# Four-layer block plus a second network on one core: in layer B, queries are scaled in the scores and rotated on VectorE, and the keys' sums of squares become two fp32r products, issued two tiles after their tile

## The chip, the cores and the metric

One core of one Trainium2 chip runs the whole program. The metric is the device time of one execution in microseconds (us); less is better. Engines: TensorE (PE, matrix products), VectorE (DVE), ScalarE (ACT), GpSimd (POOL) and SyncE (SP, which issues loads). Each works through its own instructions in order, and they hold each other back with counting semaphores.

## The reference, cut to what matters

The program computes two networks, one behind the other, on 512 tokens of width 1024. The change is in the first one's second layer, called B here: a norm, a projection, a query and key norm, partial rotation (the first 32 of 128 dimensions), attention in three groups of different windows, a gate and an output projection.

```python
def mixer_b(h, w_in, q_gain, k_gain, w_out):
    proj = h @ w_in
    qkv = proj[..., :n_qkv].reshape(bsz, S, 3, N_B_GROUPS, B_HEADS, HEAD_DIM)
    z = proj[..., n_qkv:]
    for g, (window, dilation) in enumerate(B_PATTERNS):
        q = apply_partial_rotary(rms_norm(qkv[:, :, 0, g], q_gain[g]), cos, sin)
        k = apply_partial_rotary(rms_norm(qkv[:, :, 1, g], k_gain[g]), cos, sin)
        o, lse = dilated_window_attention(q, k, qkv[:, :, 2, g], window // dilation, dilation)
    ...
    y = o.reshape(bsz, S, B_WIDTH).astype(h.dtype) * jax.nn.silu(z)
    return y @ w_out
```

rms_norm divides a vector of 128 by the root of its mean square and multiplies it with a gain. The root differs by token and head, the gain by dimension.

## The kernel before, in words

All order is written out by hand, one function for each engine. Layer B runs over i = 0 to 3, each a pair of heads. One i has these parts:

- **Twelve query and key tiles**, t = 0 to 11, with t = 4g + 2w + f: g is the group, w is 0 for queries and 1 for keys, f the head. A tile is [128 dimensions, 512 tokens], made by PE as 24 products of 512 columns in PSUM bank t mod 3 (`tile_f`; lines L558 to L560 of `mm3`: each fp32 product is three fp32r products of a high and a low part). ACT squares the tile into `sq` (L1538) and copies it to `tmp` (L1543). Behind the next tile, PE sums the squares over the 128 dimensions with one fp32 product against a matrix of ones (`ssq`, L803), ACT takes the root (L1530), DVE its reciprocal (L2154), multiplies tile, gain and reciprocal (L2159), and starts the rotation: a shuffle of 32 partitions and a product with the sine table (L2168, L2170). POOL ends it (`rope`, L420, L423).
- **Values**, six tiles of 48 products of 256 columns.
- **Attention units** n = 0 to 7, each 128 queries of one head. PE makes the scores (L843, L845). DVE adds the mask and takes the row maximum in one instruction (L2184), negates it (L2187), ACT takes the exponential (L1556), DVE divides by its sum (L2191, L2193), PE transposes the weights (`flip`, L854), ACT copies them out of PSUM (`turned`, L1566), and PE multiplies with the values (`far` L867, `close` L874). A value tile (n up to 3) or a gate tile (n = 4, 6) stands between. The last two flips stand behind tiles 0 and 1 of the next i.

ACT also writes the high part of the weights (`Wh`, L1339), POOL the low part (`Wl`, L366), two panels ahead of PE; a panel serves two tiles. SP loads the raw weights into three buffers.

## Time and profile before

| what | value |
|---|---|
| median of 3 runs | 3163.09 us (3161.67 to 3164.63) |
| the profiled execution | 3160.02 us, its span 3158.3 us |
| busy: PE, DVE, ACT, POOL | 98%, 50%, 35%, 49% of the span |
| chain that ended last, by engine | PE 92%, DVE 4%, ACT 1%, issue 1%, POOL 1%, DMA 1% |
| granted PE clock, mean | 0.992 |

The span is first to last instruction, and 1.7 us lie around it. The profiled execution is 3.1 us below the median. A granted clock of 1.00 is TensorE's level of 2.4 GHz, 0.50 that of 1.2 GHz. In the rows further down a matmul's duration runs until its last result, so that the durations of neighbours overlap; the distance of two starts tells what one costs a busy PE. An fp32 product has two records, an fp32r product or a transpose one.

### The profile page before, as it was taken

The numbers are of one execution on the slowest core, as the hardware profiler recorded it, in microseconds if no ns is written. First come the engines' busy times: TensorE is split into PE (matmuls) and PEld (weight loads), VectorE is DVE, ScalarE is ACT, GpSimd is POOL, SyncE is SP. The second block draws the span as 40 slices with busy tenths as digits, with TensorE's granted clock in tenths as the row PEclk, the third lists the DMA queues.
The fourth block names the chain that finished last, engine by engine and source line by source line (L and its number), as shares of the span: only waits on it lengthen the run. The fifth ranks groups of instructions, "written<-read, shape, count | busy, mean of one in ns | idle before, by whom it ended". The sixth has DMA issues, their size and how long they took to land.

```text
span 3158.3 us, 38137 instructions
## 1 busy us (share of the span) xinstructions
PE 3097.0 (98%) x15692; PEld 2524.9 (80%) x15692; DVE 1582.0 (50%) x2066; ACT 1100.3 (35%) x1445; POOL 1552.3 (49%) x1138
## 2 busy tenths in 40 slices
PE   8999999999999999999999999899999999999998
PEld 6888878788888888878887888676888787778887
DVE  6654475838473525355466777654211356542113
ACT  3322244444443423332223444434222343242222
POOL 4444475748473555454444422236445556354453
PEclk9999999999999999999999999899999999999999
DMA  5544322222222323355443111112333242223331
GB/s 199 169 156 159 135 83 80 80 67 81 67 81 76 98 94 103 106 185 177 136 160 117 54 41 41 41 54 94 94 106 94 81 147 80 80 67 94 105 95 67
DMA packets 270975, 319.26 MB, mean 101 GB/s; under 512 B 6850, under 2 KB 228689, under 8 KB 270482
## 3 DMA queue, kind: packets, MB, share of 16 engines
q1 hardware_dynamic: 232768, 247.48, 24.2%
q10 hardware_dynamic: 38034, 69.34, 6.5%
q8 instruction: 125, 2.05, 0.3%
q14 instruction: 48, 0.39, 0.0%
HBM read 310.50 MB, written 6.29 MB: 100 GB/s over the span
## 4 chain that ended last, share of the span: by engine, by line
PE 92%; DVE 4%; ACT 1%; issue 1%; POOL 1%; DMA 1%; ACTq 0%; SPq 0%; DVEq 0%
PE ps L558 26%; PE ps L560 25%; PE ps L559 25%; PE psx L803 1%; PE psx L1091 1%; PE ps L1122 1%; PE ps L629 1%; PE psx L782 1%; PE psx L1251 1%; PE ps L597 1%; PE psx L845 1%; POOL Wl L366 1%; PE ps L593 1%; DVE stD L2354 1%; PE ps L594 1%
## 5 line engine op out<-in xcount | busy, mean ns | idle before, releaser
L366 POOL TENSOR_TENSOR Wl<-Wr,Wh 128x512 fp32r<-128x512 f32 x928 | 1271.5, 1402 | 1407.9 <-ACT Wh L1339 1403.8
L558 PE MATMUL ps<-Ah,Wh 128*128 128x512 f32 x1944 | 778.1, 400 | 0.0
L560 PE MATMUL ps<-Ah,Wl 128*128 128x512 f32 x1944 | 757.5, 390 | 0.0
L559 PE MATMUL ps<-Al,Wh 128*128 128x512 f32 x1944 | 757.3, 390 | 0.0
L1339 ACT ACTIVATE Wh<-Wr 128x2048 fp32r<-128x2048 f32 x232 | 443.1, 1910 | 349.6 <-DMA Wr<-in_w_mlp_in_dram 109.6
L558 PEld LDWEIGHTS ps<-Ah,Wh 128*128 128x128 f32 x1944 | 365.1, 188 | 84.8 <-issue 12.0
L559 PEld LDWEIGHTS ps<-Al,Wh 128*128 128x128 f32 x1944 | 365.1, 188 | 81.9 <-issue 8.9
L560 PEld LDWEIGHTS ps<-Ah,Wl 128*128 128x128 f32 x1944 | 364.8, 188 | 77.3
L558 PE MATMUL ps<-Yh,Wh 128*128 128x512 f32 x1088 | 426.0, 392 | 0.1
L559 PE MATMUL ps<-Yl,Wh 128*128 128x512 f32 x1088 | 423.8, 390 | 0.0
L560 PE MATMUL ps<-Yh,Wl 128*128 128x512 f32 x1088 | 423.7, 389 | 0.0
L558 PEld LDWEIGHTS ps<-Yh,Wh 128*128 128x128 f32 x1088 | 204.6, 188 | 44.0 <-issue 0.8
L560 PEld LDWEIGHTS ps<-Yh,Wl 128*128 128x128 f32 x1088 | 204.5, 188 | 42.8
L559 PEld LDWEIGHTS ps<-Yl,Wh 128*128 128x128 f32 x1088 | 204.5, 188 | 41.9
L558 PE MATMUL ps<-Wh,Ah 128*128 128x256 f32 (+1 forms) x688 | 220.7, 321 | 2.2 <-DVE vA L2078 2.2
L2070 DVE SCALAR_TENSOR_TENSOR macc<-modw,sc,macc 128x512 f32<-128x512 f32 x168 | 163.5, 973 | 113.0 <-DMA modw<-in_w_mod_dram 106.6
L559 PE MATMUL ps<-Wl,Ah 128*128 128x256 f32 (+1 forms) x688 | 215.1, 313 | 0.0
L560 PE MATMUL ps<-Wh,Al 128*128 128x256 f32 (+1 forms) x688 | 215.0, 312 | 0.0
L2154 DVE RECIPROCAL rs<-rs 128x512 f32<-128x512 f32 x48 | 160.6, 3346 | 37.8 <-ACT rs L1530 37.8
L2437 DVE TENSOR_TENSOR tmp<-tmp 128x512 f32<-128x512 f32 x64 | 52.2, 816 | 201.2 <-ACT tmp L1807 201.2
L558 PEld LDWEIGHTS ps<-Wh,Ah 128*128 128x128 f32 x688 | 131.1, 191 | 13.8 <-issue 5.5
L559 PEld LDWEIGHTS ps<-Wl,Ah 128*128 128x128 f32 x688 | 131.1, 191 | 9.2 <-issue 1.9
(408 smaller groups left out, 3893.8 us busy)
## 6 DMA issues: line engine op xcount, KB each, us to landing
Wr<-in_a_w_in_dram SPq DMA_DIRECT2D x48, 1024.0 KB, 6.3
modw<-in_w_mod_dram ACTq DMA_DIRECT2D x96, 512.0 KB, 5.4
Wr<-in_b_w_in_dram SPq DMA_DIRECT2D x40, 1024.0 KB, 5.0
Wr<-in_w_mlp_in_dram SPq DMA_DIRECT2D x32, 1024.0 KB, 5.5
Wr<-in_w_mlp_out_dram SPq DMA_DIRECT2D x32, 1024.0 KB, 5.1
Wr<-in_a_w_out_dram SPq DMA_DIRECT2D x16, 1024.0 KB, 5.1
Wr<-in_c_w_in_dram SPq DMA_DIRECT2D x16, 1024.0 KB, 5.4
Wr<-in_attn_w_qkv_dram SPq DMA_DIRECT2D x12, 1024.0 KB, 5.1
```

The source lines that it names most:

```text
L366: last = pool.tensor_tensor(E.Wl[:, s, part], E.Wr[:, s, part], E.Wh[:, s, part].bitcast(F32), ALU.subtract)
L558: pe.matmul(o, ah, bh, start=first, stop=False)
L559: pe.matmul(o, ah, bl, start=False, stop=False)
L560: return pe.matmul(o, al, bh, start=False, stop=last)
L593: pe.matmul(bank[b], part(E.Wh, p, k, f * P, f * P + P, KD), Ah[:, k, :], start=(k == 0), stop=False)
L594: pe.matmul(bank[b], part(E.Wl, p, k, f * P, f * P + P, KD), Ah[:, k, :], start=False, stop=False)
L597: m = pe.matmul(bank[b], part(E.Wh, p, k, f * P, f * P + P, KD), Al[:, k, :], start=False, stop=(k == KD - 1))
L629: pe.matmul(bank[t], Ah[:, a, t * P:(t + 1) * P], part(W, p, k, 0, S, TT), start=(a == 0 and W is E.Wh), stop=False)
L1339: act.activation(E.Wh[:, s, :], E.Wr[:, s, :], ACT.Copy).then_inc(*HI.did(p))
L2070: dve.scalar_tensor_tensor(t, w, E.sc2[:, k, who:who + 1], t, ALU.mult, ALU.add).then_inc(*V.did("mac", L, nb, who, k))
L2154: dve.reciprocal(rs[:, r, :], rs[:, r, :]).then_inc(*V.did())
L2437: dve.tensor_tensor(t, t, t, ALU.mult).then_inc(*V.did(L, "sqr", iq, c))
```

## The change

**Queries.** Their tile is multiplied by the gain alone, on ACT, straight into `QB`. Rotation runs wholly on DVE (`turn_query`). For a group, the squares of both heads are summed at once behind tile 4g + 2 by eight narrow fp32 products (`query_sums`), whose result has one row of sums for each of four blocks of 128 tokens. ACT takes the root (`query_roots`), PE transposes it behind tile 4g + 3 (`columns`), DVE takes the reciprocal of 128x4 numbers (`rate`), and the attention units multiply the scores with it. So the fused mask and maximum becomes three multiply-adds and a separate maximum.

**Keys.** The square is split into an fp32r high part (ACT, `rsR`, the memory of `rs`) and low part (DVE, `square_low`), and two fp32r products sum them (`key_sum`), behind tile t + 2 rather than t + 1. Root, reciprocal, scaling (`scaled`) and rotation (`turn_key`, then POOL) follow as before. Keys 10 and 11 of an i have places of their own: `key_sum(10)` behind tile 11, `key_sum(11)` behind the first value tile. On DVE key t is scaled in the step of tile t + 3 (10 and 11: one step later).

```diff
-    E.ones, E.ident = sb("ones", [P, P]), sb("ident", [P, P])
+    E.onesR, E.ident = sb("onesR", [P, P], F32R), sb("ident", [P, P])
+    E.ones = E.onesR[:].bitcast(F32)
...
+    E.rsR, = phase(("rsR", [P, 2, S], F32R))
     E.rs = sb("rs", [P, 2, S])
+    E.sqR, = phase(("sqR", [P, 2, S], F32R))
     E.sq = sb("sq", [P, 2, S])
...
-            t = 0
             for g in range(3):
-                for qk in range(2):
-                    for f in range(2):
-                        if t:
-                            rope(i, t - 1)
-                        if f == 0:
-                            ahead("B", "qk", i, g, qk)
-                        t += 1
+                ahead("B", "qk", i, g, 0)
+                if g:
+                    rope(i, 4 * g - 2)
+                ahead("B", "qk", i, g, 1)
+                if g:
+                    rope(i, 4 * g - 1)
             for g in range(3):
+                if g == 0:
+                    rope(i, 10)
...
-        def ssq(i, t):
-            r = t % 2
-            into(4 + r)
-            pe.wait_ge(*A.of("B", "sq", i, t))
-            pe.matmul(psx[:, r, :], ones[:], sq[:, r, :], start=True, stop=True).then_inc(*X.did("B", "ssq", i, t))
-            emptied[4 + r] = A.of("B", "sqrt", i, t)
+        def key_sum(i, t):
+            b = 5 - t % 2
+            into(b)
+            pe.wait_ge(*V.of("B", "sl", i, t))
+            pe.matmul(bank[b], E.onesR[:], E.rsR[:, t % 2, :], start=True, stop=False)
+            pe.matmul(bank[b], E.onesR[:], E.sqR[:, t % 2, :], start=False, stop=True).then_inc(*X.did("B", "ssq", i, t))
+            emptied[b] = A.of("B", "sqrt", i, t)
+
+        def query_sums(i, g):
+            into(4)
+            pe.wait_ge(*A.of("B", "sq", i, 4 * g + 1))
+            for f in range(2):
+                for q in range(TT):
+                    m = pe.matmul(psx[32 * q:32 * q + 32, 0, f * P:(f + 1) * P], ones[:, 0:32], sq[:, f, q * P:(q + 1) * P], start=True, stop=True)
+            m.then_inc(*X.did("B", "ssq", i, 4 * g))
+            emptied[4] = V.of("B", "rq", i, g)
+
+        def columns(i, g):
+            pe.wait_ge(*A.of("B", "sqrt", i, 4 * g))
+            for f in range(2):
+                m = pe.transpose(psx[:, 0, (2 + f) * P:(3 + f) * P], rs[:, 1, f * P:(f + 1) * P], ident[:])
+            m.then_inc(*X.did("B", "rt", i, g))
...
-            if t:
-                ssq(i, t - 1)
+            if t % 4 == 2:
+                query_sums(i, t // 4)
+            elif t % 4 == 3:
+                if t == 11:
+                    key_sum(i, 10)
+                columns(i, t // 4)
+            elif t >= 4:
+                key_sum(i, t - 2)
...
+                pe.wait_ge(*V.of("B", "turned", i, 8 + hh))
...
-        def sqrt(i, t):
-            r = t % 2
+        def key_root(i, t):
             act.wait_ge(*X.of("B", "ssq", i, t))
-            if t >= 2:
-                act.wait_ge(*V.of("B", "qk", i, t - 2))
-            act.activation(rs[:, r, :], psx[:, r, :], ACT.Sqrt, bias=eps[:, 0:1], scale=1.0 / P).then_inc(*A.did("B", "sqrt", i, t))
+            act.activation(rs[:, t % 2, :], psx[:, 1 - t % 2, :], ACT.Sqrt, bias=eps[:, 0:1], scale=1.0 / P).then_inc(*A.did("B", "sqrt", i, t))
+
+        def query_roots(i, g):
+            act.wait_ge(*X.of("B", "ssq", i, 4 * g))
+            if g:
+                act.wait_ge(*V.of("B", "qk", i, 4 * g - 1))
+            act.activation(rs[:, 1, 0:2 * P], psx[:, 0, 0:2 * P], ACT.Sqrt, bias=eps[:, 0:1], scale=1.0 / P).then_inc(*A.did("B", "sqrt", i, 4 * g))
 
         def qk(i, t):
+            g, f = t // 4, t % 2
             act.wait_ge(*T.of("B", "qk", i, t))
-            if t >= 2:
+            if is_key(t):
+                act.wait_ge(*X.of("B", "ssq", i, 4 * g))
+            elif t >= 4:
                 act.wait_ge(*X.of("B", "ssq", i, t - 2))
             elif i:
                 act.wait_ge(*V.of("B", "y", 0, 2 * (i - 1)))
-            act.activation(sq[:, t % 2, :], ps[t % 3][:], ACT.Square).then_inc(*A.did("B", "sq", i, t))
-            if t >= 3:
-                act.wait_ge(*V.of("B", "qk", i, t - 3))
-            elif i:
-                act.wait_ge(*X.of("B", "pv", i - 1, 0))
-            act.activation(tmp[:, t % 3, :], ps[t % 3][:], ACT.Copy).then_inc(*A.did("B", "cp", i, t))
-            if t % 2 == 0:
-                ahead("B", "qk", i, t // 4, t // 2 % 2)
+            act.activation(sq[:, f, :], ps[t % 3][:], ACT.Square).then_inc(*A.did("B", "sq", i, t))
+            if is_key(t):
+                n = 2 * g + f
+                act.wait_ge(*A.of("B", "sq", i, t))
+                if f:
+                    act.wait_ge(*X.of("B", "rt", i, g))
+                elif t >= 4:
+                    act.wait_ge(*V.of("B", "qk", i, t - 4))
+                act.activation(E.rsR[:, f, :], sq[:, f, :], ACT.Copy).then_inc(*A.did("B", "sh", i, t))
+                if n >= 3:
+                    act.wait_ge(*V.of("B", "qk", i, 4 * ((n - 3) // 2) + 2 + (n - 3) % 2))
+                elif i:
+                    act.wait_ge(*X.of("B", "pv", i - 1, 0))
+                act.activation(tmp[:, n % 3, :], ps[t % 3][:], ACT.Copy).then_inc(*A.did("B", "cp", i, t))
+            else:
+                if i and t == 0:
+                    act.wait_ge(*X.of("B", "s", i - 1, 7))
+                act.activation(E.QB[:, g, f, :], ps[t % 3][:], ACT.Identity, scale=pk(E, "b_q_gain", g)).then_inc(*A.did("B", "cp", i, t))
+            if f == 0:
+                ahead("B", "qk", i, g, t // 2 % 2)
...
-                if t:
-                    sqrt(i, t - 1)
                 qk(i, t)
+                if t % 4 == 2:
+                    query_roots(i, t // 4)
+                elif t == 11:
+                    key_root(i, 10)
+                elif t >= 4 and t % 4 < 2:
+                    key_root(i, t - 2)
...
-        def rest(i, t):
-            g, qk, f, r = t // 4, t // 2 % 2, t % 2, t % 2
-            dst = (KB if qk else QB)[:, g, f, :]
+        def square_low(i, t):
+            r = t % 2
+            dve.wait_ge(*A.of("B", "sh", i, t))
+            dve.tensor_tensor(E.sqR[:, r, :], sq[:, r, :], E.rsR[:, r, :].bitcast(F32), ALU.subtract).then_inc(*V.did("B", "sl", i, t))
+
+        def rq(g, f):
+            return stB[:, B_UNITS + 2 * g + f, :]
+
+        def rate(i, g):
+            dve.wait_ge(*X.of("B", "rt", i, g))
+            for f in range(2):
+                dve.reciprocal(rq(g, f), psx[:, 0, (2 + f) * P:(3 + f) * P].rearrange("p (q n) -> p q n", q=TT)[:, :, 0]).then_inc(*V.did("B", "rq", i, g))
+
+        def scaled(i, t):
+            n, r = t // 4 * 2 + t % 2, t % 2
             dve.wait_ge(*A.of("B", "sqrt", i, t))
             dve.reciprocal(rs[:, r, :], rs[:, r, :]).then_inc(*V.did())
             dve.wait_ge(*V.now())
             dve.wait_ge(*A.of("B", "cp", i, t))
-            if i and t == 0:
-                dve.wait_ge(*X.of("B", "s", i - 1, 7))
-            dve.scalar_tensor_tensor(dst, tmp[:, t % 3, :], pk(E, "b_k_gain" if qk else "b_q_gain", g), rs[:, r, :],
+            dve.scalar_tensor_tensor(KB[:, t // 4, t % 2, :], tmp[:, n % 3, :], pk(E, "b_k_gain", t // 4), rs[:, r, :],
                                      ALU.mult, ALU.mult).then_inc(*V.did("B", "qk", i, t))
+
+        def turn_key(i, t):
             dve.wait_ge(*V.of("B", "qk", i, t))
-            if t >= 2:
-                dve.wait_ge(*G.of("B", "rope", i, t - 2))
-            elif i and t == 0:
+            if t >= 4:
+                dve.wait_ge(*G.of("B", "rope", i, t - 4))
+            elif i and t == 2:
                 dve.wait_ge(*X.of("B", "pv", i - 1, 0))
-            swapped = (acc if r else tmp[:, 3, :])[0:32, :]
+            swapped = (acc if t % 2 else tmp[:, 3, :])[0:32, :]
             pinned()
-            dve.stream_shuffle(swapped, dst[0:32, :], SWAP).then_inc(*V.did("B", "swap", i, t))
+            dve.stream_shuffle(swapped, KB[0:32, t // 4, t % 2, :], SWAP).then_inc(*V.did("B", "swap", i, t))
             dve.wait_ge(*V.of("B", "swap", i, t))
             dve.tensor_tensor(swapped, swapped, ropeB[:, 1, :], ALU.mult).then_inc(*V.did("B", "rp", i, t))
+
+        def turn_query(i, t):
+            q, swapped = QB[0:32, t // 4, t % 2, :], PB[0:32, 0, :]
+            dve.wait_ge(*A.of("B", "cp", i, t))
+            if i and t == 0:
+                dve.wait_ge(*X.of("B", "flip", i - 1, 6))
+            dve.wait_ge(*V.now())
+            pinned()
+            dve.stream_shuffle(swapped, q, SWAP).then_inc(*V.did())
+            dve.wait_ge(*V.now())
+            dve.tensor_tensor(swapped, swapped, ropeB[:, 1, :], ALU.mult).then_inc(*V.did())
+            dve.tensor_tensor(q, q, ropeB[:, 0, :], ALU.mult).then_inc(*V.did())
+            dve.wait_ge(*V.now())
+            dve.tensor_tensor(q, q, swapped, ALU.add).then_inc(*V.did("B", "turned", i, t))
...
-            pinned()
-            dve.tensor_tensor_reduce(PB[:, u % 2, :], psx[:, u % 2, :], maskB[:, u % 4, :], 1.0, 10 * NEG,
-                                     ALU.add, ALU.max, stB[:, u, 0:1]).then_inc(*V.did("B", "sc", i, u))
+            if u % 4 == 0:
+                dve.wait_ge(*V.of("B", "rq", i, 2))
+            for g, c0, c1 in ((0, 0, 256), (1, 256, 384), (2, 384, 512)):
+                dve.scalar_tensor_tensor(PB[:, u % 2, c0:c1], psx[:, u % 2, c0:c1], rq(g, u // 4)[:, u % 4:u % 4 + 1], maskB[:, u % 4, c0:c1],
+                                         ALU.mult, ALU.add).then_inc(*V.did("B", "sc", i, u))
             dve.wait_ge(*V.of("B", "sc", i, u))
+            dve.tensor_reduce(stB[:, u, 0:1], PB[:, u % 2, :], AX.X, ALU.max).then_inc(*V.did("B", "mx", i, u))
+            dve.wait_ge(*V.of("B", "mx", i, u))
...
-            for t in range(11):
-                rest(i, t)
-                if i and t == 1:
+            for t in range(13):
+                if t % 4 == 3:
+                    rate(i, t // 4)
+                if t < 12:
+                    if is_key(t):
+                        square_low(i, t)
+                    else:
+                        turn_query(i, t)
+                k = t - 1 if t > 10 else t - 3
+                if k >= 2 and is_key(k):
+                    scaled(i, k)
+                    turn_key(i, k)
+                if i and t == 2:
                     y(i - 1, 1)
-            rest(i, 11)
```

DVE around tile 5 of head pair 0, before (`rs` reciprocal, scaling, shuffle, sine product of one tile each):

```order
280 L2154 RECIPROCAL rs<-rs 128x512 [waits act]
281 L2159 SCALAR_TENSOR_TENSOR QB<-tmp,PK,rs 128x512 [waits act,dve]
282 L2168 STREAM_SHUFFLE tmp<-QB 32x512 [waits dve,pool]
283 L2170 TENSOR_TENSOR tmp<-tmp,ropeB 32x512 [waits dve]
284 L2154 RECIPROCAL rs<-rs 128x512 [waits act]
285 L2159 SCALAR_TENSOR_TENSOR QB<-tmp,PK,rs 128x512 [waits act,dve]
```

The same place after the change, from the turning of query tile 5 to the scaling of key tile 3:

```order
281 L2246 STREAM_SHUFFLE PB<-QB 32x512 [waits act,dve]
282 L2248 TENSOR_TENSOR PB<-PB,ropeB 32x512 [waits dve]
283 L2249 TENSOR_TENSOR QB<-QB,ropeB 32x512
284 L2251 TENSOR_TENSOR QB<-QB,PB 32x512 [waits dve]
285 L2221 RECIPROCAL rs<-rs 128x512 [waits act]
286 L2224 SCALAR_TENSOR_TENSOR KB<-tmp,PK,rs 128x512 [waits act,dve]
287 L2235 STREAM_SHUFFLE tmp<-KB 32x512 [waits dve]
288 L2237 TENSOR_TENSOR tmp<-tmp,ropeB 32x512 [waits dve]
289 L2208 TENSOR_TENSOR sqR<-sq,rsR 128x512 [waits act]
290 L2221 RECIPROCAL rs<-rs 128x512 [waits act]
291 L2224 SCALAR_TENSOR_TENSOR KB<-tmp,PK,rs 128x512 [waits act,dve]
```

Keys 2 and 3 are now scaled behind query tile 5, with the split of key 6's square between them, and queries have no reciprocal of 512 columns.

ACT after the change, at tile 6 of head pair 0 (root of key 3, then square, high part and copy of key 6, a weight panel's high part, and the root of group 1's queries):

```order
150 L1558 ACTIVATE rs<-psx,eps 128x512 [waits aux]
151 L1575 ACTIVATE sq<-ps 128x512 [waits aux,tile]
152 L1583 ACTIVATE rsR<-sq 128x512 [waits dve,act]
153 L1588 ACTIVATE tmp<-ps 128x512
154 L1370 ACTIVATE Wh<-Wr 128x2048 [waits raw1]
155 L1564 ACTIVATE rs<-psx,eps 128x256 [waits dve,aux]
```

PE after the change, at the end of tile 7, where before one fp32 product `L803 ... 128x512` stood:

```order
1834 L567 MATMUL ps<-Al,Wh 128x512
1835 L568 MATMUL ps<-Ah,Wl 128x512
1836 L827 MATMUL psx<-ident,rs 128x128 [waits act]
1837 L827 MATMUL psx<-ident,rs 128x128
1838 L566 MATMUL ps<-Ah,Wh 128x512 [waits act,lo]
```

The root of group 1's queries (row 155 of ACT) waits for DVE's scaling of key 3, whose reciprocal lies in the same memory, and PE's transposes (row 1836) wait for that root.

## Rows read from the trace of the kernel before

**Rows 1.** Windows, layer B: busy us and count of each engine, granted clock, DMA.

```profile
421.00:1022.00 601.00, 599.43 (x3486) 495.82 (x3487) 370.34 (x447) 260.00 (x391) 376.05 (x268) 1.00 0.23 76
```

**Rows 2.** Waits of TensorE (PE) in layer B: total us, times, longest.

```profile
PE psx L854 <- DVE PB L2193: 1.1, 4, 0.3
```

**Rows 3.** Timeline of PE, head pair 0: start us, us, what.

```profile
434.11 1.02 PE L803 MATMUL psx<-sq,ones 128*128 128x512 f32 x2
...
435.20 0.40 PE L559 MATMUL ps<-Al,Wh 128*128 128x512 f32 x1
...
440.46 1.02 PE L803 MATMUL psx<-sq,ones 128*128 128x512 f32 x2
```

**Rows 4.** Timeline of PE at full clock: narrow fp32 products, then transposes.

```profile
2146.12 0.64 PE L678 MATMUL psx<-sq,ones 128*32 128x128 f32 x16
2146.69 1.98 PE L1005 MATMUL psx<-hsF,tabF 128*128 128x512 f32 x4
...
546.54 0.60 PE L854 MATMUL psx<-ident,PB 128*128 128x128 f32 x4
546.98 0.61 PE L867 MATMUL ps<-PTB,VB 128*128 128x128 f32 x4
```

**Rows 5.** Timeline of ScalarE (ACT), head pair 0.

```profile
454.21 0.69 ACT L1530 ACTIVATE rs<-psx,eps 128x512 f32<-128x512 f32 x1 [4.68 <-PE psx L803]
454.79 0.59 ACT L1538 ACTIVATE sq<-ps 128x512 f32<-128x512 f32 x1
455.27 0.60 ACT L1543 ACTIVATE tmp<-ps 128x512 f32<-128x512 f32 x1
```

**Rows 6.** Timeline of VectorE (DVE), head pair 0.

```profile
484.21 1.02 DVE L2159 SCALAR_TENSOR_TENSOR QB<-tmp,PK,rs 128x512 f32<-128x512 f32 x1
...
486.20 0.68 DVE L2170 TENSOR_TENSOR acc<-acc,ropeB 32x512 f32<-32x512 f32 x1
486.81 3.33 DVE L2154 RECIPROCAL rs<-rs 128x512 f32<-128x512 f32 x1
```

**Rows 7.** Groups of DVE: count, busy us, mean ns, idle before.

```profile
L2154 DVE RECIPROCAL rs<-rs 128x512 f32<-128x512 f32 x48 | 160.6, 3346 | 37.8 <-ACT rs L1530 37.8
L2023 DVE TENSOR_TENSOR Yl<-tmp,Yh 128x512 fp32r<-128x512 f32 x112 | 88.6, 791 | 58.9 <-ACT Yh L1813 46.2 <-ACT Yh L1650 11.2
L2354 DVE TENSOR_REDUCE stD<-psx 128x2 f32<-128x1536 f32 x32 | 56.2, 1755 | 34.2 <-PE psx L1091 34.2
...
L2159 DVE SCALAR_TENSOR_TENSOR QB<-tmp,PK,rs 128x512 f32<-128x512 f32 x24 | 26.9, 1123 | 0.9
```

**Rows 8.** Tile QB: min/median/max ns of one.

```profile
L2159 DVE SCALAR_TENSOR_TENSOR QB<-tmp,PK,rs x24: 750/1018/1868, 427.6 to 909.7; 128x512 f32<-128x512 f32 x24
```

**Rows 9.** Attention unit 4: DVE's first step, then PE's transposes.

```profile
534.33 0.69 DVE L2184 CUSTOM_DVE_ANT_0 PB<-psx,maskB 128x512 f32<-128x512 f32 x1 [4.67 <-PE psx L845]
...
536.93 0.63 PE L854 MATMUL psx<-ident,PB 128*128 128x128 f32 x4 [0.28 <-DVE PB L2193]
```

**Rows 10.** ACT's copy of unit 6 and PE's product that reads it.

```profile
558.03 0.60 ACT L1566 ACTIVATE PTB<-psx 128x512 f32<-128x512 f32 x1
...
561.75 0.61 PE L867 MATMUL ps<-PTB,VB 128*128 128x128 f32 x4
```

**Rows 11.** PE after long and short waits, and the granted clock of 2 us.

```profile
2018.46 2.26 PE L1091 MATMUL psx<-KD,QD 64*128 64x512 f32 x8 [3.02 <-ACT rs L1737]
2020.65 2.52 PE L1122 MATMUL ps<-tmp,VD 128*128 128x128 f32 x12
...
2020.00:2022.00 2.00, 2.00 (x10) 1.35 (x7) 1.24 (x1) 0.00 (x0) 0.00 (x0) 0.50 0.89 231
...
2051.12 1.13 PE L1161 MATMUL ps<-woF,hdX 64*128 64x512 f32 x2 [1.41 <-DVE kcF L2382]
2052.30 1.56 PE L1091 MATMUL psx<-KD,QD 64*128 64x512 f32 x8
...
2055.33 1.50 PE L1122 MATMUL ps<-tmp,VD 128*128 128x128 f32 x12
```

More of the change, by code:

```diff
@@ L2035, in preamble @@
     def preamble():
[L2036 removed]
+        dve.memset(E.acc[:], 1.0).then_inc(*V.did())
+        dve.wait_ge(*V.now())
+        dve.tensor_copy(E.onesR[:], E.acc[:, 0:P]).then_inc(*V.did("ones"))
         dve.memset(eps[:], EPS).then_inc(*V.did("eps"))
```

20 lines of the change are left out of this document (11 added, 9 removed).

## Prediction

> **What bounds the kernel now.** I read the page first: the chain that ended last lies almost wholly on PE. Then the windows, for the stretch that the change touches: in the 601 us of layer B, PE is busy for 599.4 at a granted clock of 1.00, while DVE has 370 us of work and POOL 376 [rows 1]. Then the waits: the largest one of PE there is the flip that waits for DVE's division, 1.1 us over four times [rows 2]. So nothing but PE's own instructions sets the time of this layer. Work taken from PE there is time gained, us for us, and a wait put on PE is time lost in the same way. Work taken from DVE, ACT or POOL gains nothing by itself.
>
> **Keys: one fp32 product becomes two fp32r ones.** Two sums start 6.35 us apart (434.11 and 440.46). From the tile's second product at 435.20 to the next sum are 23 products in 5.26 us [rows 3], 0.229 each, so a tile is 5.49 and one fp32 sum 0.86. Two fp32r products of the same 512 columns are 0.46. There are 24 keys: 24 x 0.40 = **9.6 us gained**.
>
> **Queries.** A group loses two fp32 sums, 1.72 us. It gets eight fp32 products with 32 result rows and 128 columns, for which the norm has the very form: eight took from 2146.12 to 2146.69, 0.57 us at full clock. It also gets two transposes; four took 0.44 us (546.54 to 546.98) [rows 4], so 0.22. Saved 0.93, and 12 groups give **11.1 us gained**. The preamble's fp32r ones and the moved mask load lie beside loads and the layer's norm, and I cost them at nothing; if all of the one copy of 128 columns showed, it would be under 1 us [rows 8].
>
> **The new wait behind tile 7 and tile 11.** The transposes of group g wait for the root of the queries' sums. That root waits (g at least 1) until DVE has scaled key 4g - 1. I follow this from the end of tile 5 (e5 = 0), in the order that the listing of DVE after the change shows.
>
> - PE: key sum 0.46, tile 6 5.49, query sums 0.57, tile 7 5.49. PE is at the transposes at **12.0**.
> - ACT: after the key sum's last result (0.46 + 0.16 until it has drained) come square and copy of query 5, started 0.48 apart and the last 0.60 long [rows 5]: the copy is there at 1.70.
> - DVE turns query 5: shuffle and sine product as before, cosine product and sum new. Before, 0.97 lay between a multiplication's end (485.23) and the sine product (486.20), and 0.61 from there to the next start [rows 6]. I split the 0.97 into a wait of DVE for itself, 0.20, and a shuffle of 0.77; a product that the next one waits for I take at its 0.68 and 0.07 of latency. I take 0.77 + 0.61 + 0.75 + 0.61 = 2.74, so 4.44.
> - DVE scales key 2: reciprocal 3.35 and 0.04 of latency, multiplication 1.12 [rows 7]: 8.95. It rotates it: from the multiplication's end at 485.23 to the next reciprocal at 486.81 are 1.58 [rows 6]: 10.53.
> - It splits the square of key 6, a subtraction to fp32r as L2023, 0.79 [rows 7], of which 0.75 until the next starts: 11.28. (ACT's high part waits for key 2's scaling at 8.95, and is there in time.)
> - It scales key 3: 3.36 and 1.12, so 15.76. ACT takes the root of 256 columns; 512 take 0.69 [rows 5], I take 0.50 and 0.08 of latency: **16.34**.
>
> PE waits 16.34 - 12.0 = 4.3 us behind tile 7. Behind tile 11 the same chain runs from the end of tile 9, and PE has one key sum more (0.46): 3.9 us. Queued behind the waiting transposes is everything that PE has, next the tile after. Group 0 has no such wait, since its root waits for no key. Four i make 4 x 8.2 = **32.9 us lost**. The bounds of one wait: with the shortest multiplication (0.75 [rows 8]) for both multiplications and the subtraction it is 3.6 and 3.1; with the longest (1.87) for the three it is 6.9 and 6.4. I take the means, since POOL runs beside DVE here as before. Over four i: 27 to 53 us.
>
> The Trainium skill (GPSIMD Engine Reference, Key points) says that GpSimd shares its SBUF interfaces with VectorE and that instructions with two SBUF inputs contend. By that rule the spread from 0.75 to 1.87 is POOL's doing, and the change takes the queries' rotations from POOL. With the shortest durations throughout, the lost time would be 27.
>
> **The clock after such waits.** PE waited 3.02 us before 2018.46, and then the granted clock was 0.50, the level of 1.2 GHz: the scores took 2.26 and the products after them 2.52, where the same took 1.56 and 1.50 at full clock [rows 11]. That is 1.7 us lost. After a wait of 1.41 (2051.12) the next scores took 1.56, so the clock held [rows 11]. The new waits are longer than 3, and full-size products follow, so I expect a fall each time. A part of it should lie inside the longer wait, so I take 1.35 for each, between 0 and 1.7: 8 x 1.35 = **10.8 us lost** (0 to 14).
>
> The Trainium skill (TensorE: Matmul & The Clock Gate, What's actually happening) says that the throttled clock is the default and that activity releases it. By it, too, idle time costs more than its own length; without it the sum would be 10.8 lower.
>
> **Attention units.** The fused instruction took 0.69 for 512 columns [rows 9]; a maximum over 1536 columns took 1.755 [rows 7]. That is 1.04 ns a column and 0.16 fixed. Three pieces are then 1.01, the wait of DVE for itself 0.20, the maximum 0.69: 1.9 instead of 0.7, less 0.1 in which the pieces overlap, so **1.1 us longer**, bounds 0.8 and 1.6. Most units have a tile beside them on PE. The flip of unit 4 has not: it stood 0.28 us waiting already [rows 9], so here all of it shows: 4 x 1.1 = **4.4 us lost**. Units 6 and 7 together make ACT's copies at the head of the next i some 2.0 later, and PE comes 0.86 sooner, since the sum behind tile 1 is gone. The copy that started at 558.03 ended 3.1 us before PE's product at 561.75 [rows 10], so 0.2 is left. I cost it at 0, with up to 2 us for three such places.
>
> **The sum**, against the profiled execution: 3160.0 - 9.6 - 11.1 + 32.9 + 10.8 + 4.4 = 3187.4, that is +27.4. The runs' median is 3.1 above that execution, so 3190.5 in its terms.
>
> **What lies beside the path.** DVE has in a group two turned queries (5.5), two splits (1.6), two scaled and rotated keys (12) and the small reciprocals, under 20 us, against some 24 of PE: it is not the bound, only late in its order. ACT gets a copy for each key (0.6). POOL loses 48 of its 96 rotation steps and keeps the weights' low parts; it waits more for keys, but a panel has over 20 us. SP's queue is not touched. The values behind tile 11 hide key 11: its sum stands one value tile behind, and two more follow before unit 0 needs it.
>
> **The rivals.**
>
> - The waits, but no fall of the clock (0.12). PE's work before and after is dense. Against it: 3.02 us sufficed once. Time 3190.5 - 10.8 = 3179.7.
> - The chain on DVE is longer than its means (0.14). For it: key 3's multiplication falls where POOL makes a panel's low part. Time: +15 to +20 for waits near the upper bound, near 3208.
> - **Faster** (0.08): the chain never stands on PE's path. It is one mechanism: key 3 scaled before PE is at the transposes. That needs a chain 4.3 us shorter, as if DVE scaled key 2 ahead of query 5, whose copy comes 1.7 us after its tile while DVE idles. The order rows speak against it. Time 3163.1 - 20.7 + 4.4 = 3146.8. It decides at a wait of 16.3 / 8 = 2.0 us: below that, with no fall of the clock, the kernel is faster.
> - The waits come out between (0.05), about 2 us each, and the change cancels: 3163.
>
> **How the numbers follow.** The forecast itself gets 0.61; its own range is 3180 to 3202 (waits 4 us more or less over an i, clock 0 to 14). For 8 in 10 I go from 3170, the no-fall case with the shortest chain, to 3209. A difference of 0.2%, 6.3 us, is about the least that can be told from none here. Slower by more than that: 0.61 + 0.12 + 0.14 and a little of the cases between, 0.88. Faster 0.08, same 0.04.
>
> **What would show it.** In the profile after: eight waits of PE on ACT's root in front of the transposes, about 4 us each, none in group 0; granted clock under 1.00 after them in layer B; key sums at 0.46 and query sums at 0.57 to 0.6; four waits of a flip on DVE near 1.4. Wrong if those eight waits are under 2 us, or if the clock stays at 1.00.

## The result, and the profile after

Before, the kernel took 3163.86 us (median of 4 runs, 3161.67 to 3167.15), after the change 3211.82 us (4 runs, 3211.60 to 3213.44): a ratio of 1.0155, 95% interval 1.0142 to 1.0167. The change makes it **slower by 48.0 us**. I had forecast slower by 27.4, with a range up to 3209. The sign was right and the size was not: the time lies outside the range. The profiled execution of after took 3213.44 us (span 3211.7). The same kernel in a later comparison took 3207.88 beside 3166.17, which is 41.7 us slower; that time would lie just inside the range.

The page of after, engines' busy time and the shares of the chain that ended last:

```profile
PE 3104.2 (97%) x15860; PEld 2539.0 (79%) x15860; DVE 1590.4 (50%) x2179; ACT 1109.1 (35%) x1457; POOL 1489.9 (46%) x1090
...
PE 88%; DVE 7%; issue 1%; ACT 1%; POOL 1%; DMA 1%; ACTq 0%; SPq 0%; DVEq 0%
```

Before, 92% of the chain was PE's and 4% DVE's; now it is 88% and 7%. So the end now depends on DVE's work in places where it depended on PE's. To place them, I take the norm's products with ones, which stand once at the end of each part of the program, and read when they start. First before, then after (PE's timeline: start, us, line, operation; a count under x20 means only that the window asked for ended inside the group, and the start is not touched by it):

```profile
400.64 2.39 PE L649 MATMUL psx<-ones,ident 128*128 128x128 f32 x20
...
1022.48 2.39 PE L649 MATMUL psx<-ones,ident 128*128 128x128 f32 x20
...
1335.56 2.39 PE L649 MATMUL psx<-ones,ident 128*128 128x128 f32 x20
...
2766.86 1.39 PE L649 MATMUL psx<-ones,ident 128*128 128x128 f32 x11
```

```profile
402.41 2.39 PE L657 MATMUL psx<-onesR,ident 128*128 128x128 f32 x20
...
1067.25 1.95 PE L657 MATMUL psx<-onesR,ident 128*128 128x128 f32 x16
...
1380.34 1.83 PE L657 MATMUL psx<-onesR,ident 128*128 128x128 f32 x15
...
2821.09 2.17 PE L657 MATMUL psx<-onesR,ident 128*128 128x128 f32 x18
```

From the first row to the second is layer B: 621.8 us before, 664.8 after, so **43.0 us longer**. From the third row to the fourth no line of the program differs, yet it is 1431.3 before and 1440.8 after. Most of that isn't the change: the same kernel's second profile has 1431.8 there, and the kernels of the experiments lie anywhere from 1432 to 1441. It goes with the time for which the granted clock stood at its lower level in this stretch: 44.4 us in after, 23.9 in its second profile. So profiled spans differ by some 9 us outside of layer B, and I compare layer B. (Some 3 us may be the change's even so, see the end of the part on the prediction.)

PE's waits in layer B of after (waiting tile and line, who releases it: us in all, times, longest):

```profile
PE psx L827 <- ACT rs L1564: 36.9, 8, 5.6
PE psx L885 <- DVE PB L2278: 4.5, 4, 1.1
PE psx L811 <- DVE sqR L2208: 2.6, 4, 0.7
```

Where [rows 2] had 1.1 us of waiting over four flips, there are eight waits of the transposes (L827) on the root of the queries' sums (L1564), 36.9 us, up to 5.6 each. They stand behind tile 7 and tile 11, for the four i, and none in group 0, as forecast. The flips wait 4.5, or 1.12 each, where I had said near 1.4. Not forecast: the sum of key 10 waits 0.65 four times for the split of its square on DVE.

PE's timeline of after in the first i shows the terms that I had priced (sums L811 and L820, transposes L827; tiles left out):

```profile
428.80 0.65 PE L820 MATMUL psx<-sq,onesR 128*32 128x128 f32 x16
...
435.00 0.38 PE L827 MATMUL psx<-ident,rs 128*128 128x128 f32 x2
...
440.71 0.39 PE L811 MATMUL psx<-rsR,onesR 128*128 128x512 f32 x1
...
446.64 0.39 PE L811 MATMUL psx<-rsR,onesR 128*128 128x512 f32 x1
...
452.65 0.64 PE L820 MATMUL psx<-sq,onesR 128*32 128x128 f32 x16
...
464.58 0.69 PE L827 MATMUL psx<-ident,rs 128*128 128x128 f32 x2 [5.57 <-ACT rs L1564]
```

From one key sum to the next (440.71 to 446.64) are 5.93 us where [rows 3] had 6.35: 0.42 gained, 24 times 10.1. The query sums and the tile behind them take 6.20 (428.80 to 435.00), the two transposes and a tile 5.71 (435.00 to 440.71), a key sum and a tile 5.93. The end of tile 5 is at 446.64, tile 6 and the key sum end at 452.65, and the transposes of group 1 start at 464.58, after 5.57 us of waiting.

What was late is read from DVE, ACT and POOL in the same stretch (rows of after's timeline, DVE first):

```profile
448.74 0.73 DVE L2246 STREAM_SHUFFLE PB<-QB 32x512 f32<-32x512 f32 x1
449.50 1.28 DVE L2248 TENSOR_TENSOR PB<-PB,ropeB 32x512 f32<-32x512 f32 x1
...
452.03 3.33 DVE L2221 RECIPROCAL rs<-rs 128x512 f32<-128x512 f32 x1
455.39 0.75 DVE L2224 SCALAR_TENSOR_TENSOR KB<-tmp,PK,rs 128x512 f32<-128x512 f32 x1
...
456.69 0.73 DVE L2235 STREAM_SHUFFLE tmp<-KB 32x512 f32<-32x512 f32 x1 [0.37 <-issue]
...
458.06 1.77 DVE L2208 TENSOR_TENSOR sqR<-sq,rsR 128x512 fp32r<-128x512 f32 x1
459.77 3.33 DVE L2221 RECIPROCAL rs<-rs 128x512 f32<-128x512 f32 x1
463.14 0.82 DVE L2224 SCALAR_TENSOR_TENSOR KB<-tmp,PK,rs 128x512 f32<-128x512 f32 x1
```

```profile
456.24 0.64 ACT L1583 ACTIVATE rsR<-sq 128x512 fp32r<-128x512 f32 x1 [2.21 <-DVE KB L2224]
...
464.05 0.48 ACT L1564 ACTIVATE rs<-psx,eps 128x256 f32<-128x256 f32 x1 [4.88 <-DVE KB L2224]
```

```profile
457.50 1.79 POOL L428 TENSOR_TENSOR KB<-KB,ropeB 32x512 f32<-32x512 f32 x1 [7.26 <-DVE tmp L2235]
...
460.93 5.84 POOL L374 TENSOR_TENSOR Wl<-Wr,Wh 128x512 fp32r<-128x512 f32 x4
```

Key 3's multiplication (463.14, 0.82) ends at 463.96, ACT takes the root at 464.05, PE's transposes follow. Backwards from there: key 3's reciprocal starts at 459.77 because the split before it took 1.77 us, with POOL's rotation of key 2 (457.50 to 459.29) beside it. The sine product at 449.50 took 1.28 where others take 0.68.

The granted clock over this wait (windows of 2 us; columns: length, busy us and instructions of PE, PEld, DVE, ACT, POOL, then mean granted clock, DMA share, GB/s):

```profile
460.00:462.00 2.00, 0.00 (x0) 0.00 (x0) 2.00 (x1) 0.00 (x0) 2.00 (x2) 1.00 0.88 284
462.00:464.00 2.00, 0.00 (x0) 0.00 (x0) 1.92 (x2) 0.00 (x0) 2.00 (x3) 0.54 0.68 240
464.00:466.00 2.00, 1.42 (x5) 1.23 (x6) 1.64 (x5) 1.60 (x4) 2.00 (x2) 0.50 0.00 0
466.00:468.00 2.00, 2.00 (x6) 1.57 (x5) 1.29 (x1) 0.48 (x1) 2.00 (x2) 0.50 0.00 0
468.00:470.00 2.00, 2.00 (x8) 1.58 (x7) 0.00 (x0) 0.00 (x0) 1.73 (x2) 0.75 0.04 8
```

PE stands from 459.01 to 464.58. The clock is still 1.00 in the first 3 us of that, 0.54 and 0.50 from 462 on, and 1.00 again at 469. PE's products from 464.58 on run at the level of 1.2 GHz for 4.4 us. Over layer B I added up the windows of 0.5 us: PE is busy for 2.7 to 6.1 us at the low level behind each of the eight waits, and half of that, **17.3 us**, is lost. Another 1.7 us are lost in the norm at the layer's start (407.6 to 411.0), behind none of these waits; the second profile lacks them and loses 16.8, all behind the eight. So the clock takes 19.0 in all here. Before, it stood at 1.00 in all of layer B.

Together in layer B: 18.6 gained by the cheaper sums, 39.5 lost by waits (36.9 + 2.6), 3.4 by the flips (4.5 less 1.1), 19.0 by the clock. That is +43.3, against 43.0 read.

### The profile page after: what moved, and what is told of

It reads as the page before. It is cut to its first block, busy times and chain, and to the rows that moved or that the text cites. A ratio compares the mean times of both kernels' runs of the same rounds, so it can differ in the third digit from the quotient of the medians.

```text
span 3211.7 us, 38480 instructions
## 1 busy us (share of the span) xinstructions
PE 3104.2 (97%) x15860; PEld 2539.0 (79%) x15860; DVE 1590.4 (50%) x2179; ACT 1109.1 (35%) x1457; POOL 1489.9 (46%) x1090
## 3 DMA queue, kind: packets, MB, share of 16 engines
q1 hardware_dynamic: 232768, 247.48, 23.9%
q8 instruction: 126, 2.06, 0.3%
## 4 chain that ended last, share of the span: by engine, by line
PE 88%; DVE 7%; issue 1%; ACT 1%; POOL 1%; DMA 1%; ACTq 0%; SPq 0%; DVEq 0%
PE ps L566 25%; PE ps L568 24%; PE ps L567 24%; DVE rs L2221 2%; PE psx L1122 1%; PE ps L1153 1%; PE ps L637 1%; PE psx L790 1%; PE psx L1282 1%; PE psx L876 1%; PE ps L605 1%; PE psx L874 1%; PE ps L601 1%; POOL Wl L374 1%; PE ps L602 1%
## 5 line engine op out<-in xcount | busy, mean ns | idle before, releaser
L566 PE MATMUL ps<-Ah,Wh 128*128 128x512 f32 x1944 | 770.1, 396 | 1.2 <-DVE vA L2133 1.2
L568 PEld LDWEIGHTS ps<-Wh,Al 128*128 128x128 f32 x688 | 134.2, 195 | 7.6
```

The lines of the kernel that those rows point to most:

```text
L566: pe.matmul(o, ah, bh, start=first, stop=False)
L568: return pe.matmul(o, al, bh, start=False, stop=last)
```

## The experiments

Two theories stood at first. The main one: PE's loss is a wait on DVE's in-order work, which the change makes PE depend on because the queries' root is written into the memory of a key's reciprocal, and the low clock behind each wait. The rival: DVE's order alone is at fault, since query 5 stands ahead of key 2.

**The root in memory of its own.** The queries' root of groups 1 and 2 goes into a tile that holds the gate later, so it doesn't wait for key 4g - 1 to be scaled. ACT's rows have only the waits that the other tile needs: the high part of keys 7 and 11, too, no longer waits for the transposes (not shown below).

```diff
-                m = pe.transpose(psx[:, 0, (2 + f) * P:(3 + f) * P], rs[:, 1, f * P:(f + 1) * P], ident[:])
+                m = pe.transpose(psx[:, 0, (2 + f) * P:(3 + f) * P], (E.szB[:] if g else rs[:, 1, :])[:, f * P:(f + 1) * P], ident[:])
...
-            if g:
-                act.wait_ge(*V.of("B", "qk", i, 4 * g - 1))
-            act.activation(rs[:, 1, 0:2 * P], psx[:, 0, 0:2 * P], ACT.Sqrt, bias=eps[:, 0:1], scale=1.0 / P).then_inc(*A.did("B", "sqrt", i, 4 * g))
+            if g == 1 and i:
+                act.wait_ge(*V.of("B", "y", 0, 2 * i - 1))
+            elif g == 2:
+                act.wait_ge(*X.of("B", "rt", i, 1))
+            act.activation(E.szB[:, 0:2 * P] if g else rs[:, 1, 0:2 * P], psx[:, 0, 0:2 * P], ACT.Sqrt, bias=eps[:, 0:1], scale=1.0 / P).then_inc(*A.did("B", "sqrt", i, 4 * g))
```

> The root of the queries' sums of groups 1 and 2 goes to memory of its own, so it no longer waits for the scaling of key 4g - 1; nothing else changes. Theory 1 (the eight waits on this root, and the clock that falls behind them, are the loss): the 37 us of waits and about 17 us of clock go, granted clock in layer B 1.00, time near 3158 (between 3153 and 3165). Rival (VectorE's whole work in a group is what PE waits for, and the root is only the place where it shows): the waits come back at the key sums or at the tiles' banks, and at least half of the 54 us stays, time above 3180.

Measured: 3170.11 (10 runs, 3166.21 to 3176.55), 1.0021 of before (1.0012 to 1.0030). 41.7 of the 48 us are gone by the medians, and layer B is 628.3. So most of the loss hangs on the shared memory, and the rival falls with the next kernel. But the time is 12 us above the 3158 that I expected (7.5 above before), and the waits of PE say why:

```profile
PE psx L811 <- ACT szB L1566: 11.2, 4, 3.1
PE psx L885 <- DVE PB L2280: 4.5, 4, 1.1
```

The wait for DVE moved, in part, to the sum of key 10. The profile names ACT's root (L1566) for it, but nothing in `key_sum` waits for that root. It waits for the split of the key's square on DVE, which ends at the same time: in the first i at 484.08, the root at 484.12. PE goes on 0.15 behind the split, as in after (491.15 and 491.30). With one more such wait of 1.0 and 2.3 on the root itself PE waits 14.5 in front of these sums and transposes, where it was 39.5, and the clock still loses 6.3 us. That part is what the rival of my expectation had said. DVE was late by its two-input steps. PE, then the timeline of DVE, then POOL:

```profile
484.23 0.47 PE L811 MATMUL psx<-rsR,onesR 128*128 128x512 f32 x1 [1.90 <-ACT szB L1566]
```

```profile
467.84 1.81 DVE L2251 TENSOR_TENSOR QB<-QB,ropeB 32x512 f32<-32x512 f32 x1
...
474.22 1.76 DVE L2251 TENSOR_TENSOR QB<-QB,ropeB 32x512 f32<-32x512 f32 x1
...
482.33 1.75 DVE L2210 TENSOR_TENSOR sqR<-sq,rsR 128x512 fp32r<-128x512 f32 x1
...
609.91 6.74 DVE L2251 TENSOR_TENSOR QB<-QB,ropeB 32x512 f32<-32x512 f32 x1
```

```profile
609.51 1.62 POOL L431 TENSOR_TENSOR KB<-KB,acc 32x512 f32<-32x512 f32 x1
611.10 5.01 POOL L374 TENSOR_TENSOR Wl<-Wr,Wh 128x512 fp32r<-128x512 f32 x4
```

In the first i, products over 32x512 that take 0.68 to 0.72 elsewhere take 1.47 to 1.81, beside POOL's work. In each of the other three i the cosine product of query 8 takes 6.74 to 6.75 us. It starts while POOL adds, lasts through POOL's next four steps, which take 1.27 to 1.28 each (others of them take up to 1.8), and ends 0.5 us after the last of them. These three steps stand ahead of the three waits of 3.1. Why a step is held up for one of POOL's steps here and for five there, no run shows.

**Only DVE's order.** The scaling and rotation of key t - 3 are issued ahead of the query, the shared memory stays.

```diff
             for t in range(13):
+                k = t - 1 if t > 10 else t - 3
+                if k >= 2 and is_key(k):
+                    scaled(i, k)
+                    turn_key(i, k)
                 if t % 4 == 3:
...
-                k = t - 1 if t > 10 else t - 3
-                if k >= 2 and is_key(k):
-                    scaled(i, k)
-                    turn_key(i, k)
```

> In each step VectorE scales and rotates the key before it turns the query or splits a square, rather than after. Memory and waits are as in the changed kernel. Theory 1 with the order on VectorE as the cause: the root is there 5 us sooner, so the eight waits shrink from 3.9 to 5.6 us to at most 1 each and the clock stays at 1.00: 3160 to 3168. Rival (length of VectorE's work): the waits stay above 3 us each and the time above 3195.

Measured: 3209.54 (3207.14 to 3218.74), 1.0152 (1.0135 to 1.0169), layer B 666.7. PE's waits:

```profile
PE psx L811 <- DVE sqR L2208: 30.7, 8, 5.8
PE psx L827 <- ACT rs L1564: 11.9, 4, 3.0
```

42.6 us of waits instead of 39.5. The root's waits fell from 36.9 to 11.9, and the key sums now wait 30.7 for the split, which the early scaling pushed back. The clock loses 16.9. So the order is not the cause by itself: whichever of DVE's steps stands last is the one PE waits for.

**PE kept busy before the waits.** Sixteen products that nobody reads stand in front of the transposes of groups 1 and 2. They cost PE nearly what it waits, so they show what the clock alone takes.

```diff
         def columns(i, g):
+            if g:
+                into(3)
+                for k in range(16):
+                    pe.matmul(bank[3], part(E.Wh, E.at["B", "qk", i, g, 1], k % KD, 0, P, KD), Ah[:, k % KD, :], start=True, stop=True)
```

> Before the transposes of groups 1 and 2, PE makes 16 products of 512 columns into an unused bank (3.7 us, no one reads them), so that the wait is filled with work. The root still comes when it came. Theory 1: the waits shrink by 3.7 each, the clock stays at 1.00, and only the clock's part is gained: 3211.8 - 17 = 3195 (3192 to 3199). Rival (the low clock costs next to nothing, the waits are all): 3209 to 3213.

Measured: 3195.28 (3191.84 to 3198.79), 1.0101 (1.0086 to 1.0116), as expected; layer B 650.6. The windows view over nearly all of it:

```profile
424.00:1052.00 628.00, 612.46 (x3774) 514.87 (x3773) 377.05 (x558) 266.19 (x401) 315.31 (x220) 1.00 0.22 73
```

The granted clock is 1.00 as a mean, 1.7 us are lost to it instead of 19.0, and the kernel is 16.5 us faster (14.2 in layer B) with products that do nothing. The waits on the root fell from 36.9 to 8.4. By these numbers the products cost about 31.6 of PE's time, an estimate (28.5 + 17.3 less 14.2), so 3 more than they took off the waits. The Trainium skill (TensorE: Matmul & The Clock Gate, What's actually happening) says that TensorE is throttled by default and released by activity; this trace agrees, by those 16.5 us.

**The scores not scaled.** The three scaled pieces and their maximum go back to one fused instruction. This kernel leaves out the queries' scale.

```diff
-            for g, c0, c1 in ((0, 0, 256), (1, 256, 384), (2, 384, 512)):
-                dve.scalar_tensor_tensor(PB[:, u % 2, c0:c1], psx[:, u % 2, c0:c1], rq(g, u // 4)[:, u % 4:u % 4 + 1], maskB[:, u % 4, c0:c1],
-                                         ALU.mult, ALU.add).then_inc(*V.did("B", "sc", i, u))
+            pinned()
+            dve.tensor_tensor_reduce(PB[:, u % 2, :], psx[:, u % 2, :], maskB[:, u % 4, :], 1.0, 10 * NEG,
+                                     ALU.add, ALU.max, stB[:, u, 0:1]).then_inc(*V.did("B", "sc", i, u))
```

> The attention units keep the fused mask and maximum of the kernel before, so the queries' scale is left out of the scores; all else is the changed kernel. Theory 1: the flip of unit 4 waits 0.28 instead of 1.12 us, four times, so 3.4 us less: 3208.4 (3206 to 3210). Rival (the longer units cost more than that wait, by delaying the next head pair): 6 to 12 us less, below 3206.

Measured: 3200.46 (3195.20 to 3204.17), 1.0112 (1.0095 to 1.0129). The time is 8 us below what I expected, and lies in the rival's band. Layer B is 658.8, so 6.1 less: the flips wait 0.28 again, four times, which is the 3.4 of my sum, and the clock loses 15.2 instead of 19.0. The waits on the root are 36.8 as in after, so the rival's delay of the next head pair isn't there. The rest of the 11 us lies outside of layer B, where executions differ without a change. So 3.4 is shown for the flips, and no more.

**Key rotation on POOL cut to one column.** One execution. This kernel leaves out all but one column of the cosine product and sum of the keys.

```diff
-        pool.tensor_tensor(q, q, E.ropeB[:, 0, :], ALU.mult).then_inc(*G.did("B", "cos", i, t))
+        pool.tensor_tensor(q[:, 0:1], q[:, 0:1], E.ropeB[:, 0, 0:1], ALU.mult).then_inc(*G.did("B", "cos", i, t))
...
-        pool.tensor_tensor(q, q, spare, ALU.add).then_inc(*G.did("B", "rope", i, t))
+        pool.tensor_tensor(q[:, 0:1], q[:, 0:1], spare[:, 0:1], ALU.add).then_inc(*G.did("B", "rope", i, t))
```

> The changed kernel, in which POOL's two steps of the keys' rotation work on one column instead of 512 (so the keys' rotation is left out for the rest). Theory 1 with contention between VectorE and POOL in two-input steps: the subtraction that splits a key's square behind a rotation takes 0.7 instead of 1.8 us, and the eight root waits shrink by about 1 us each, to about 29 in all. Rival (the subtraction to fp32r takes 1.3 to 1.8 by itself): waits and durations unchanged.

Measured: 3205.54, layer B 661.6. The split of a square (by its tile: shortest, median and longest in ns), first in after, then in this kernel:

```profile
L2208 DVE TENSOR_TENSOR sqR<-sq,rsR x24: 692/1292/1789, 433.4 to 955.7; 128x512 fp32r<-128x512 f32 x24
```

```profile
L2208 DVE TENSOR_TENSOR sqR<-sq,rsR x24: 671/693/1765, 431.8 to 951.0; 128x512 fp32r<-128x512 f32 x24
```

The median falls from 1292 to 693 ns when POOL has next to nothing to do beside it. So the contention is shown for this step. The Trainium skill (GPSIMD Engine Reference, Key points) says that instructions of VectorE with two SBUF inputs contend with GpSimd; the trace agrees. The 2.6 us of waits for key 10's split are gone. But PE's waits on the root did not fall, they sum to 39.0 (8 times, up to 5.1), and my 29 was wrong. The chain's other two-input step took the delay over. DVE and then POOL, one i later:

```profile
608.91 0.67 DVE L2208 TENSOR_TENSOR sqR<-sq,rsR 128x512 fp32r<-128x512 f32 x1
...
612.88 1.79 DVE L2224 SCALAR_TENSOR_TENSOR KB<-tmp,PK,rs 128x512 f32<-128x512 f32 x1
```

```profile
610.42 5.38 POOL L374 TENSOR_TENSOR Wl<-Wr,Wh 128x512 fp32r<-128x512 f32 x4 [0.79 <-ACT Wh L1370]
```

The split takes 0.67 now, but POOL comes to the low parts of a weight panel at 610.42 instead of 613.07, and key 3's multiplication, which lies among them, takes 1.79 instead of 0.82. An overlap doesn't always slow DVE: in after the same multiplication lies beside the same weights' low parts (460.93 on) and takes 0.82, while the four of POOL take 5.84 instead of 5.38. Which of the two is slowed I can't predict from these rows.

**Three variants on top of the root's own memory.** Each is compared with its 3170.11, layer B 628.3.

The query's cosine product and sum go to POOL, as they were before the change:

```diff
+                rope(i, 4 * g)
+                rope(i, 4 * g + 1)
...
-            dve.tensor_tensor(swapped, swapped, ropeB[:, 1, :], ALU.mult).then_inc(*V.did())
-            dve.tensor_tensor(q, q, ropeB[:, 0, :], ALU.mult).then_inc(*V.did())
-            dve.wait_ge(*V.now())
-            dve.tensor_tensor(q, q, swapped, ALU.add).then_inc(*V.did("B", "turned", i, t))
+            dve.tensor_tensor(swapped, swapped, ropeB[:, 1, :], ALU.mult).then_inc(*V.did("B", "rp", i, t))
```

> As e1_own (roots in memory of their own), and the queries' cosine product and sum go back to POOL. Layer B took 628.3 us in e1_own, 6.5 above before, with 11 us of waits on the key sums of keys 10 that came late from VectorE. Theory 1 (VectorE is late because its two-input steps of 32x512 take up to 1.8 us beside POOL): two such steps less for each query, the waits fall under 3 us, the clock stays at 1.00, layer B 612 to 618. Rival (POOL becomes late with the weights' low parts or the keys' rotation): PE waits on POOL, layer B above 628.

Measured: 3159.72 (10 runs, 3151.73 to 3161.45), 0.9982 (0.9972 to 0.9992), layer B 612.5, as expected. The waits of key 10's sum are gone, and no step of the queries' turn is longer than 1.80. I had expected less than 3 us of waits; what is left is the flips and, 1.0 each time, the sum of key 11:

```profile
PE psx L886 <- DVE PB L2281: 4.5, 4, 1.1
PE psx L813 <- DVE sqR L2211: 4.1, 4, 1.0
```

The keys' sum as one fp32 product again, with no split on DVE:

```diff
-            pe.wait_ge(*V.of("B", "sl", i, t))
-            pe.matmul(bank[b], E.onesR[:], E.rsR[:, t % 2, :], start=True, stop=False)
-            pe.matmul(bank[b], E.onesR[:], E.sqR[:, t % 2, :], start=False, stop=True).then_inc(*X.did("B", "ssq", i, t))
+            pe.wait_ge(*A.of("B", "sq", i, t))
+            pe.matmul(bank[b], ones[:], sq[:, t % 2, :], start=True, stop=True).then_inc(*X.did("B", "ssq", i, t))
```

> As e1_own, but keys are summed by one fp32 product of 0.86 us again, at the new place two tiles behind; the high and low parts of the squares are gone from ACT and VectorE. Theory 1: PE loses 24 x 0.40 = 9.6 us, and gains the 11 us of waits and 6 of clock back, since VectorE has 24 subtractions of 1.3 us less and ACT no longer waits for a key's scaling: layer B 619 to 623. Rival (the fp32r products are worth their VectorE work): layer B above 628.

Measured: 3163.38 (10 runs, 3154.71 to 3164.45), 0.9995 (0.9985 to 1.0005), layer B 616.1, a little better than expected. It gives back the 10 us that the fp32r pair had gained on PE, and yet it is 12 us shorter in layer B than with them, since no wait but the flips' 4.5 is left and the clock stays at 1.00. This kernel also drops ACT's high part of the square and its wait for DVE, so by itself it doesn't tell which of these helped. The kernel before it keeps both. So either load taken from DVE, the queries' rotation or the split with its high part, ends the waits of key 10's sum; with both DVE is late.

The second gate tile moved ahead of unit 4's flip:

```diff
-                elif n % 2 == 0:
-                    gate(i, n // 2 - 2)
+                elif n == 4:
+                    gate(i, 0)
                 scores(i, n)
+                if n == 5:
+                    gate(i, 1)
```

> As e1_own, and the second gate tile stands ahead of the flip of unit 4 instead of behind it, so that this flip has a tile beside its longer chain. Expected: the four waits of 1.12 us go, layer B 623.8 (623 to 625). Rival (the wait moves to the flip of unit 5, whose chain now starts later): 628 again.

Measured: 3169.53 (10 runs, 3160.70 to 3172.65), 1.0018 (1.0007 to 1.0028). The median shows nothing against 3170.11. Layer B is 621.9, or 6.4 less, and the waits of the flips are gone. They were worth 4.5; the clock loses 5.0 there instead of 6.3.

**The best of them.** The root's own memory, the query's rotation on POOL, and the moved gate tile together:

> e6_pool and e8_gate together: roots in memory of their own, the queries' cosine product and sum on POOL, the second gate tile ahead of the flip of unit 4. Theory 1: the flip waits of 4.5 us go from e6_pool's layer B of 612.5, so 608 (607 to 610), some 14 us under before; time near 3152. Rival (POOL or the flip of unit 5 takes the wait over): 612 again, time near 3157.

Measured: 3151.52 (5 runs, 3146.77 to 3153.72), 0.9955 of before (0.9941 to 0.9968), where before took 3166.17 in the same comparison; layer B 607.1 against 621.8. Its windows view over most of layer B, and its only wait of PE over 1 us in sum there:

```profile
424.00:1000.00 576.00, 571.70 (x3609) 483.54 (x3608) 332.19 (x507) 261.39 (x397) 368.46 (x264) 1.00 0.24 78
```

```profile
PE psx L813 <- DVE sqR L2213: 4.1, 4, 1.0
```

PE is busy for 571.7 of 576 us at a clock of 1.00. So this version beats both kernels: the change's own gains on PE are real, and they are kept once nothing stands in front of them.

The kernel of the change was run once more beside it:

> The changed kernel once more. Layer B 664.8 again, within 3 us, since its waits are fixed by dependences and only the length of the low-clock stretches can differ. The stretch from the end of layer C to the last norm, which took 1440.8 us against 1431.3 before, differs between executions of one kernel: 1431 to 1441 in any. Rival (the change costs there too): 1440 or more again, with e10_best, which has the same code there, also at 1440.

Measured: 3207.88 (4 runs, 3201.12 to 3211.61), 1.0134 (1.0120 to 1.0148), layer B 663.6 with waits of 36.9, 4.5 and 2.5. The loss in layer B is the same within 1.3 us.

## Why the prediction was right in sign and wrong in size

**What bounds the kernel.** Right. PE sets the layer's time, and what was taken from it or put on it came out in the time.

**Keys.** 9.6 forecast, 10.1 measured.

**Queries.** 11.1 forecast, about 8.5 measured. From 428.80 to 440.71 are 11.91 us for the query sums, the transposes and two tiles. The tiles alone are 2 x 5.49, so sums and transposes take 0.93, and the stretch of a key sum that ends at the query sums (446.64 to 452.65) is 0.08 longer than that between two key sums. That is 1.01 a group where I had 0.79: the transposes took 0.22 as priced, and the eight products with 32 result rows took 0.71 in their place, not the 0.57 of [rows 4]. 1.72 less 1.01, twelve times, is 8.5. The cheaper sums together gave 18.6, not 20.7.

**The new wait.** Place, number, releaser and the absence in group 0 were right. The step that was mis-sized is this one: "It splits the square of key 6, a subtraction to fp32r as L2023, 0.79". It took 1.77 beside POOL's rotation. I had taken the mean of 112 steps elsewhere in the program, with a median of 0.69. The same trace has that line in layer B as well, three times at 1.8 (the first at 576.48), which the price leaves out. Along the chain (from the end of tile 5) the deviations are: copy of query 5 at 1.90 instead of 1.70; query 5 turned at 5.39 instead of 4.44, for 0.6 of which the sine product of 1.28 stands; key 2 scaled 9.50 instead of 8.95; split's start 11.42 instead of 10.53, with 0.37 before a shuffle that I had left out; split's end 13.13 instead of 11.28; key 3 scaled 17.32 instead of 15.76. The multiplications, which I had priced at 1.12, took 0.75 and 0.82 and gave 0.7 back. The root is done at 17.89 instead of 16.34, and PE waits 5.57, not 4.3. Over all i it is 36.9 against 32.9, inside of my bounds of 27 to 53. The wait of key 10's sum, 2.6, I had put at nothing without a reason: I had checked the split's due time for the root only, not for the sum that reads it.

**The clock.** This is the step that failed: the term that left its own bounds. "1.35 for each, between 0 and 1.7" came from [rows 11], one wait of 3.02, and made 0 to 14 us. Measured: 17.3 / 8 = 2.2 each, between 1.4 and 3.1, with 2.7 to 6.1 us of low-clock work behind a wait; 16.8 in the second profile. That the clock falls each time was right; that the price of one shorter wait bounds that of a longer one was not. The trace of before already had a dearer case, 10.2 us at the low level with PE busy throughout (2032.84 to 2043.08), so 5.1 us lost. PE kept busy gave 16.5 back, so the size is shown. Why the low clock lasts longer behind one wait than another is not.

**Attention.** 4.4 forecast; the waits are 4.5, of which 1.1 was there before, so 3.4. The pieces and the maximum were priced well, 1.00 for the three and 0.69:

```profile
545.69 1.00 DVE L2267 SCALAR_TENSOR_TENSOR PB<-psx,stB,maskB 128x256 f32<-128x256 f32 x3 [3.65 <-PE psx L876]
546.72 0.69 DVE L2270 TENSOR_REDUCE stB<-PB 128x1 f32<-128x512 f32 x1
```

From the first piece to the negation (547.44) are 1.75 where 0.73 stood before, so 1.02 more, but the first piece starts 0.75 behind the scores' last group of products (544.94) instead of 0.94, and 0.84 of it reaches the wait. Units 6 and 7 made no wait, as forecast.

**The rivals.** "No fall of the clock" did not happen. "The chain on DVE is longer than its means" did: 3208 was its time, and 3211.82 and 3207.88 were measured. But its price was not the whole excess, and that its number lies near is in good part luck: of the 15.9 us between my terms and the measured ones in layer B, 8.2 are the clock's (6.5 behind the waits, 1.7 in the norm), 6.6 the waits', 2.1 the queries' and keys' sums', and the attention gave 1.0 back. "Faster" needed key 3 to be scaled before PE is at the transposes; it became true only when the root no longer waited for that key. Its text named DVE's order as the way to it, and the experiment with that order alone refutes it.

**The remaining 5 us** between 43.0 in layer B and 48.0 in the medians lie outside of the change's stretch. The two profiled executions are 53.4 apart: 1.8 ahead of layer B (0.1 in the second profile, 0.4 to 1.6 in the experiments' kernels; whether the preamble, which I had put at nothing, has a part in it isn't shown), 43.0 in it, 9.4 in the long stretch, and 0.8 less at the end. In that stretch the length follows the time at the lower clock level: with the change's code 1431.8 and 1432.1 us at 23.9 us of it, 1434.2 at 30.7, 1440.5 to 1441.0 at 44.4. Before took 1431.3 at 30.7, so some 3 us less at the same time of low clock, and 1.0 to 1.4 of them are one wait for a table's load (1.2 before, 2.0 to 2.6 in every kernel with the change). So the clock makes most of the 9.4 (6.5 from 30.7 to 44.4), and a few us may be the change's. Why the clock is low there for longer in one execution than in another stays open.

## What to carry to other kernels

When a step goes into memory that another engine's late step still holds, the engine that bounds the kernel comes to depend on the whole in-order queue behind it: here a tile of its own for one 256-column root was worth 42 of 48 us, and reordering that queue 2. A wait put on a PE-bound stretch costs its own length and, here, about half as much again at the low clock behind it (17.3 for 36.9). Price VectorE's steps with two SBUF inputs by rows that have GpSimd busy beside them, and check a new step's due time for every reader it has. Read a wait's releaser against the program's own waits: two events 0.04 us apart can be mistaken for each other. And read a layer in every one of its rounds: the 6.7 us step stands in three of four.
